# Decay products on four row groups, modulation sums in later blocks, and linear attention's first inputs loaded during neighbourhood attention

## The reference

```python
shift_x, scale_x, gate_x = jnp.split(silu_c @ w_ada[l] + b_ada[l], 3, axis=-1)   # modulation
...
def gla_log_decay(z, w_a, b_a):              # z: (B, L, 16), w_a: (16, 192)
    g = (z @ w_a + b_a).astype(jnp.float32)
    return split_heads(jax.nn.log_sigmoid(g) / GLA_TAU, GLA_HEADS)
...
def step(state, inp):                        # gated linear attention, chunks of 64 tokens
    qi, ki, vi, gi = inp
    b = jnp.cumsum(gi, axis=2)
    q_dec, k_dec = qi * jnp.exp(b), ki * jnp.exp(-b)
    a = jnp.where(tri, jnp.einsum('bhtk,bhsk->bhts', q_dec, k_dec), 0.0)
    o = jnp.einsum('bhts,bhsv->bhtv', a, vi) + jnp.einsum('bhtk,bhkv->bhtv', q_dec, state)
    ...
```

## Time and profile before

| | us |
|---|---|
| median of three executions | 4718.71 |
| the profiled execution | 4721.0 |
| its span | 4719.2 |
| TensorE busy | 4208.3 (89%) |
| VectorE busy | 2202.5 (47%) |
| ScalarE busy | 1482.8 (31%) |
| GpSimd busy | 465.4 (10%) |

### The profile page before, as it was taken

How to read it: one execution, slowest core, us unless ns; L and a number is a source line. 1 busy time by engine, 2 the same in 40 slices (tenths; PEclk the granted TensorE clock), 3 DMA queues, 4 the chain that set the end, 5 groups by cost and what they waited for, 6 DMA issues and landing times. The chain is left out here.

```text
span 4719.2 us, 67376 instructions
## 1 busy us (share of the span) xinstructions
PE 4208.3 (89%) x25867; PEld 3358.5 (71%) x25867; DVE 2202.5 (47%) x4748; ACT 1482.8 (31%) x3341; POOL 465.4 (10%) x497
## 2 busy tenths in 40 slices
PE   7999999799669899999979956959999989979799
PEld 4777789577457778778857745847777767758687
DVE  5553111266656553111126665853831256657554
ACT  4001333156412220144316631431111257641211
POOL 3111000200000030000020000031420000100100
PEclk9999999999759999999989976979999999989899
DMA  4343121710325442212180043532111123346321
GB/s 179 118 132 112 72 72 54 262 42 13 127 101 200 171 151 69 94 72 72 58 273 14 14 151 125 219 148 78 63 65 64 61 84 118 96 156 256 116 75 64
DMA packets 230291, 520.88 MB, mean 110 GB/s; under 512 B 46587, under 2 KB 100747, under 8 KB 220627
## 3 DMA queue, kind: packets, MB, share of 16 engines
q1 hardware_dynamic: 206068, 434.47, 25.9%
q0 software_dynamic: 23904, 82.11, 4.8%
HBM read 320.07 MB, written 196.43 MB: 109 GB/s over the span
## 5 line engine op out<-in xcount | busy, mean ns | idle before, releaser
L72 PE MATMUL tm_tacc<-tm_tw_hi,hT_hi 128*128 128x384 f32 (+1 forms) x1120 | 418.6, 374 | 1.6 <-POOL tm_tw_lo L916 1.6
L73 PE MATMUL tm_tacc<-tm_tw_lo,hT_hi 128*128 128x384 f32 (+1 forms) x1120 | 413.4, 369 | 0.0
L74 PE MATMUL tm_tacc<-tm_tw_hi,hT_lo 128*128 128x384 f32 (+1 forms) x1120 | 413.3, 369 | 0.0
L72 PE MATMUL tz_tacc<-tz_tw_hi,hT_hi 128*128 128x512 f32 x896 | 359.8, 402 | 24.4 <-DVE tz_tw_lo L892 12.8
L72 PE MATMUL cm_acc<-hT_hi,cm_wb_hi 128*128 128x512 f32 (+1 forms) x912 | 362.0, 397 | 0.0
L73 PE MATMUL tz_tacc<-tz_tw_lo,hT_hi 128*128 128x512 f32 x896 | 356.1, 397 | 0.0
L74 PE MATMUL tz_tacc<-tz_tw_hi,hT_lo 128*128 128x512 f32 x896 | 356.1, 397 | 0.0
L74 PE MATMUL cm_acc<-hT_hi,cm_wb_lo 128*128 128x512 f32 (+1 forms) x912 | 344.0, 377 | 0.0
L73 PE MATMUL cm_acc<-hT_lo,cm_wb_hi 128*128 128x512 f32 (+1 forms) x912 | 343.5, 377 | 0.0
L804 DVE SCALAR_TENSOR_TENSOR tm_ds<-tm_dg,tm_ds 128x512 f32<-128x512 f32 (+1 forms) x40 | 25.6, 639 | 531.8 <-ACT tm_ds L798 531.8
L72 PEld LDWEIGHTS tm_tacc<-tm_tw_hi,hT_hi 128*128 128x128 f32 x1120 | 213.6, 191 | 56.5 <-ACT tm_tz L940 23.2
(11 more groups left out here) (370 smaller groups left out, 8801.2 us busy)
## 6 DMA issues: line engine op xcount, KB each, us to landing
scr_z<-tz_tz SPq DMA_DIRECT2D x112, 256.0 KB, 2.0
scr_zcm<-cm_zo SPq DMA_DIRECT2D x96, 256.0 KB, 2.0
scr_ztm<-tm_tz SPq DMA_DIRECT2D x68, 256.0 KB, 2.0
out_mx<-scr_mix SPq DMA_DIRECT2D x34, 512.0 KB, 3.6
out_gt<-scr_ztm SPq DMA_DIRECT2D x34, 512.0 KB, 4.5
scr_xres<-out_x POOLq DMA_DIRECT2D x34, 512.0 KB, 4.1
scr_z<-out_xn POOLq DMA_DIRECT2D x34, 512.0 KB, 4.7
cm_area<-in_w_ada POOLq DMA_DIRECT2D x64, 256.0 KB, 3.1
```

The source lines that it names most:

```text
L72: nc.tensor.matmul(out, ah, bh, start=start, stop=False)
L73: nc.tensor.matmul(out, ah, bl, start=False, stop=False)
L74: return nc.tensor.matmul(out, al, bh, start=False, stop=stop)
```

## The change

There are three parts.

1. `DecaySums`: the four products of a segment (two directions, two groups of heads) are issued together, each on its own 16 rows starting at partitions 0, 32, 64 and 96, into four banks. `pe` does so only at the first unit of a segment. Rank rows and weights lie twice on the partitions for it. Units stand one tile later (`+ 1` in `at`). The rank rows of the next segment are loaded after the first store of a segment. `load` asks for the rank rows first.
2. `Modulation`: it starts at block 26 with a period of 4 blocks instead of block 9 with 6, so its steps come after the rotated chunks. Three blocks of a period have 3, 3 and 2 steps; before, four blocks had 2 each. The row is added in the same block as the first steps.
3. `LinearInputs`: decay sums and keys of group 0 and all values are loaded into memory set aside at the right end, by SP in `neighbourhood_phase`, between the stores of output tiles 1 and 2. `gla_phase` loads the rest: queries of group 0 first, then the mask, then group 1.

```diff
 class Modulation:
-        self.start, self.period = 9, 6
+        self.start, self.period = 26, 4
...
     def dve(self, dve, n):
         j, p = (n - self.start) // self.period, (n - self.start) % self.period
-        if p == 2 and 1 <= j <= self.NG:
+        if p == 1 and 1 <= j <= self.NG:
             self.row(dve, j - 1)
-        if 0 <= j < len(self.chunks) and p >= 2:
-            self.step(dve, j, 2 * p - 4)
-            self.step(dve, j, 2 * p - 3)
+        if 0 <= j < len(self.chunks) and p >= 1:
+            for k in range(3 * p - 3, min(3 * p, KC)):
+                self.step(dve, j, k)
...
 class DecaySums:
-        self.at = {sum(tiles[:c]) + 3 * j: 5 * c + j for c in range(4) for j in range(5)}
+        self.at = {sum(tiles[:c]) + 3 * j + 1: 5 * c + j for c in range(4) for j in range(5)}
...
     def ranks(self, sp, seg):
         a, w = 512 * seg, min(512, LT - 512 * seg)
         if seg:
-            sp.wait_ge(self.g_mm, 4 * seg)
-        for d in range(2):
-            sp.dma_start(self.z[32 * d:32 * d + RANK, 0:w], rank_rows(self.io)[d, :, a:a + w]).then_inc(self.z_in, 16)
+            sp.wait_ge(self.g_mm, seg)
+        for j in range(4):
+            sp.dma_start(self.z[32 * j:32 * j + RANK, 0:w], rank_rows(self.io)[j % 2, :, a:a + w]).then_inc(self.z_in, 16)
...
     def store(self, sp, u):
...
-        if u % 4 == 3 and u < 19:
+        if u % 4 == 0 and u < 16:
             self.ranks(sp, u // 4 + 1)
 
     def pe(self, pe, u):
-        hh, d, a, w = self.place(u)
+        if u % 4:
+            return
         if u == 0:
-            pe.wait_ge(self.c_in, 48)
+            pe.wait_ge(self.c_in, 64)
         else:
             pe.wait_ge(self.g_ev, u)
-        pe.wait_ge(self.z_in, 32 * (u // 4 + 1))
-        self.nc.tensor.matmul(self.bank[:, 0:w], self.wa[32 * d:32 * d + RANK, hh * 128:(hh + 1) * 128],
-                              self.z[32 * d:32 * d + RANK, 0:w], start=True, stop=True).then_inc(self.g_mm, 1)
+        pe.wait_ge(self.z_in, 64 * (u // 4 + 1))
+        w = self.place(u)[3]
+        for j in range(4):
+            last = self.nc.tensor.matmul(self.bank[j][:, 0:w], self.wa[32 * j:32 * j + RANK, :], self.z[32 * j:32 * j + RANK, 0:w], start=True, stop=True)
+        last.then_inc(self.g_mm, 1)
...
 def neighbourhood_phase(nc, l, io, keep, na, pre):
...
                 for i, t in enumerate(tiles):
+                    if i == 2:
+                        pre.load(sp, io)
                     sp.wait_ge(o_ev, i + 1)
...
 def gla_phase(nc, l, io, keep, wo, pre):
...
-                for hh in range(2):
-                    sp.dma_start(qd[hh][0][:, :], decay_sums(io, hh, 0)).then_inc(b_in[hh][0], 16)
...
+                sp.dma_start(q[0][:, 0:LQ], io["zcm"][8, :, 0:LQ]).then_inc(q_in[0], 16)
+                for cc in range(2):
+                    sp.dma_start(mask[64 * cc:64 * cc + 64, :, :],
+                                 io["gla_mask"][64 * cc:64 * cc + 64, :, 64 * cc:64 * cc + 64]).then_inc(m["cst_in"], 16)
+                sp.dma_start(qd[1][0][:, :], decay_sums(io, 1, 0)).then_inc(b_in[1][0], 16)
+                sp.dma_start(k[1][:, :], io["zcm"][11, :, :]).then_inc(k_in[1], 16)
+                sp.dma_start(qd[1][1][:, :], decay_sums(io, 1, 1)).then_inc(b_in[1][1], 16)
+                sp.dma_start(q[1][:, 0:LQ], io["zcm"][9, :, 0:LQ]).then_inc(q_in[1], 16)
...
+class LinearInputs:
...
+    def load(self, sp, io):
+        sp.dma_start(self.sums[0][:, :], decay_sums(io, 0, 0)).then_inc(self.sums_in[0], 16)
+        sp.dma_start(self.k[:, :], io["zcm"][10, :, :]).then_inc(self.keys_in, 16)
+        sp.dma_start(self.sums[1][:, :], decay_sums(io, 0, 1)).then_inc(self.sums_in[1], 16)
+        sp.dma_start(self.v[:, :, :], io["ztm"][:, 1024 + D_NA:TM].rearrange("(t p) c -> p t c", p=128)).then_inc(self.values_in, 16)
```

More of the change, by code:

```diff
@@ L743, in __init__ @@
         self.nc, self.l, self.io = nc, l, io
-        self.z, self.wa, self.ba = P.sb("dz", [64, 512]), P.sb("dwa", [64, 256]), P.sb("dba", [128, 4])
+        self.z, self.wa, self.ba = P.sb("dz", [128, 512]), P.sb("dwa", [128, 128]), P.sb("dba", [128, 4])
         self.start, self.g, self.s = P.sb("dstart", [128, 512]), P.sb("dg", [128, 512]), P.sb("ds", [128, 512])
-        self.bank = P.ps("dbank")
+        self.bank = [P.ps(f"dbank{j}") for j in range(4)]
         (self.c_in, self.z_in, self.g_mm, self.g_ev, self.ln_ok, self.b_ok, self.b_out) = [P.sem(n) for n in (
             "dc_in", "dz_in", "dg_mm", "dg_ev", "dln_ok", "db_ok", "db_out")]
-        self.at = {sum(tiles[:c]) + 3 * j: 5 * c + j for c in range(4) for j in range(5)}
+        self.at = {sum(tiles[:c]) + 3 * j + 1: 5 * c + j for c in range(4) for j in range(5)}
     def place(self, u):
@@ L757, in ranks @@
         if seg:
-            sp.wait_ge(self.g_mm, 4 * seg)
-        for d in range(2):
-            sp.dma_start(self.z[32 * d:32 * d + RANK, 0:w], rank_rows(self.io)[d, :, a:a + w]).then_inc(self.z_in, 16)
+            sp.wait_ge(self.g_mm, seg)
+        for j in range(4):
+            sp.dma_start(self.z[32 * j:32 * j + RANK, 0:w], rank_rows(self.io)[j % 2, :, a:a + w]).then_inc(self.z_in, 16)
     def load(self, sp):
         l, io = self.l, self.io
-        sp.dma_start(self.wa[:, :], io["w_alpha"][l:l + 1, :, :].rearrange("a p n -> p (a n)")).then_inc(self.c_in, 16)
+        self.ranks(sp, 0)
+        for hh in range(2):
+            sp.dma_start(self.wa[64 * hh:64 * hh + 64, :], io["w_alpha"][l:l + 1, :, hh * 128:(hh + 1) * 128].rearrange("a p n -> p (a n)")).then_inc(self.c_in, 16)
         sp.dma_start(self.ba[:, :], io["b_alpha"][l:l + 1, :, :].rearrange("a p n -> p (a n)")).then_inc(self.c_in, 16)
         sp.dma_start(self.start[:, :], io["chunk_start"][:, 0:512]).then_inc(self.c_in, 16)
-        self.ranks(sp, 0)
     def store(self, sp, u):
@@ L1376, in gla_phase @@
         q = [P.sb(f"q{j}", [128, LT]) for j in range(2)]
-        k = [P.sb(f"k{j}", [128, LT]) for j in range(2)]
-        v = P.sb("v", [128, NT, GH * GDV])
-        qd = [wo.buf[0:2], [P.sb(f"qd1{d}", [128, LT]) for d in range(2)]]
+        pre.beside(P)
+        k = [pre.k, P.sb("k1", [128, LT])]
+        v = pre.v
+        qd = [pre.sums, [P.sb(f"qd1{d}", [128, LT]) for d in range(2)]]
         kd = [wo.buf[2:4], [P.sb(f"kd1{d}", [128, LT]) for d in range(2)]]
@@ L1404, in steps_needed @@
             return max(order[0].index(2 * n + 1), order[1].index(2 * n))
-        names = ("cst_in", "v_in",
+        names = ("cst_in",
                  "ls_ok", "exp_q", "exp_k", "qd_ok", "kte_ok", "kt_mm", "kt_ev", "u_mm", "s_ok", "a_mm", "a_ok", "o_mm", "o_ok")
         m = {n: P.sem(n) for n in names}
-        b_in = [[P.sem(f"b{hh}{d}_in") for d in range(2)] for hh in range(2)]
-        q_in, k_in = [[P.sem(f"{n}{hh}_in") for hh in range(2)] for n in ("q", "k")]
+        b_in = [pre.sums_in, [P.sem(f"b1{d}_in") for d in range(2)]]
+        q_in, k_in = [P.sem(f"q{hh}_in") for hh in range(2)], [pre.keys_in, P.sem("k1_in")]
         o_out = [P.sem(f"o_out{j}") for j in range(2)]
@@ L1653, in _, with __init__, place, behind @@
                     values_out(NO + n)
+class LinearInputs:
+    def __init__(self, P, nc):
+        self.sums_in = [P.sem(f"sums{d}_in") for d in range(2)]
+        self.keys_in, self.values_in = P.sem("keys_in"), P.sem("values_in")
+        self.nc = nc
+    def place(self, P):
+        self.sums = self.behind(P, "sums")
+        self.k, self.v = self.beside(P)
+    def behind(self, P, name):
+        return [self.nc.alloc_sbuf_tensor(f"{P.name}_{name}{d}", [128, LT], F32, side="right") for d in range(2)]
+    def beside(self, P):
+        return (self.nc.alloc_sbuf_tensor(f"{P.name}_k0", [128, LT], F32, side="right"),
+                self.nc.alloc_sbuf_tensor(f"{P.name}_v", [128, NT, GH * GDV], F32, side="right"))
+    def load(self, sp, io):
[3 more added lines that the diff above has]
+        sp.dma_start(self.v[:, :, :], io["ztm"][:, 1024 + D_NA:TM].rearrange("(t p) c -> p t c", p=128)).then_inc(self.values_in, 16)
 class OutputWeights:
-    def __init__(self, P):
-        self.buf = [P.sb(f"buf{j}", [128, LT]) for j in range(4)]
+    def __init__(self, P, pre):
+        self.buf = pre.behind(P, "buf") + [P.sb(f"buf{j}", [128, LT]) for j in (2, 3)]
         self.raw = [self.buf[k // 2][:, (k % 2) * D:(k % 2 + 1) * D] for k in range(KC)]
@@ L2840, in first_layer @@
                            [512, 512, 384, 384], [ACT.Silu] * 2 + [ACT.Copy] * 2, tiles, decays=DecaySums(P, nc, l, io, tiles))
-    with phase(nc, f"nain{l}") as P:
-        na = Neighbourhood(P, last)
-        fourier_phase(nc, l, io, keep, na)
-        neighbourhood_phase(nc, l, io, keep, na)
-    with phase(nc, f"wo{l}") as P:
-        wo = OutputWeights(P)
-        gla_phase(nc, l, io, keep, wo)
-        out_phase(nc, l, io, keep, wo)
+    with phase(nc, f"pre{l}") as Q:
+        pre = LinearInputs(Q, nc)
+        with phase(nc, f"nain{l}") as P:
+            na = Neighbourhood(P, last)
```

(7 more changed lines are left out.)

19 lines of the change are left out of this document (5 added, 14 removed).

## The result

Four executions of the changed kernel took 4635.1 to 4649.8 us, median 4641.7. The kernel before, run beside it, took 4718.4 (median of four). The ratio is 0.9835 (95% interval 0.9804 to 0.9865): 76.6 us faster, where 72.0 were forecast. The profiled execution is the longest of the four, 4649.8 us with a span of 4647.9, so the two traces differ by only 71.3 us.

What follows compares the result with a forecast made beforehand. TensorE bounds projections and neighbourhood attention, a ScalarE-VectorE-TensorE chain linear attention. Terms 26.9 + 16.8 + 8 + 20.3 = 72.0 us off the median 4718.7 give 4646.7 us; range 4632 to 4668.

Steps and rivals of the forecast that it cites:

- Part 1, packs: Projection stages: a pack of four decay products costs 1.3 us, about one single unit; 26.9 us gained over both layers.
- The start: Start of each token projection: first tile goes ahead of the decay unit and ends 1.0 us earlier per layer.
- The boundaries of the chunks: Projections, three units per layer: TensorE still waits for the weight split, which doesn't move; 3.75 us counted as not gained.
- Part 1, rank rows: Projections: waits for late rank rows and the low clock behind them go; 16.8 us gained, at least 9.
- Part 2: Modulation in the first layer's channel projection: later steps remove waits and low clock; 8 us gained, bounds 0 and 12.
- The wait ahead of block 31: Modulation, first chunk: two rotations and a short block make TensorE wait about 3 us.
- The later waits: Modulation, reductions after the first: TensorE waits 0 to 0.3 us at each.
- The 15 us to be won: Channel projection, blocks 9 to 59: 15 us of waits and low clock, nearly all in blocks 15 to 33.
- Part 3: Linear attention's inputs: chain of states starts 10.7 and 9.6 us earlier in the two layers; 20.3 us gained, at least 12.
- Cover: Early loads under neighbourhood attention, DMA engines used for 9%: they cost nothing; bounds 0 and 8 us per layer.
- Rivals 1 to 5: 1 packs paired/in-turn 0.12; 2 modulation gains nothing 0.09; 3 loads delay attention 0.08; 4 start given back 0.07; 5 slower 0.02.
- The fifth: Modulation: weights land one at a time, a step takes some 5 us, kernel slower at 4813 us; chance 0.02.

## Why the prediction was right, point by point

- **Part 1, packs: 26.9 forecast, 30.8 measured** (the changed kernel against single products with early rows, one trace each). The core was right: a unit gives back 1.25 us and a pack costs 1.26 or 1.27. The start was mis-sized. The first tile ends 2.5 and 2.6 us earlier behind the stage's start (against the kernel before 1.8 and 2.2), where 1.0 was forecast: 3.1 us more in the two layers. The boundaries of the chunks, forecast as unchanged, held in the first layer but for 0.4 us (tiles 17 and 18 take 13.28 us after and 13.25 before, tiles 53 and 54 10.75 and 10.73). In the second layer they cost 2.3 us more at two of three and 0.3 less at the third, as VectorE's scan delays the split; the forecast took it for granted that the split doesn't move. The last part, 2.6 us, isn't the change's: plain tiles of 384 columns take 4.16 or 4.24 us, in either kernel, and the trace with single products has more of the latter. Errors of both signs cancel here in part.
- **Part 1, rank rows: 16.8 forecast, 15.5 measured** by the kernel that has this edit alone; its two starts are 1.1 us longer, without which it would be 16.6. That the loss hangs on the wait and not on the unit held: with the waits gone, no half clock stands behind a single unit. But how much clock a wait costs differs between executions. In the second execution of the kernel before the same four places lose 13.9 us, as the two waits of 2.3 us in its second layer have no half clock behind them at all:

```profile
2200.91 1.09 PE L783 MATMUL tm_dbank<-tm_dz,tm_dwa 16*128 16x512 f32 x2 [2.35 <-DMA tm_dz<-scr_branch]
...
2200.90:2208.70 7.80, 7.79 (x41) 7.04 (x42) 0.00 (x0) 2.16 (x4) 0.00 (x0) 1.00 0.07 25
```

- **Part 2: 8 forecast, 5.9 between the two traces.** The wait ahead of block 31 is 2.8 us by the weight loads, 3 was forecast. The later waits were laid out as 0 to 0.3 us each and came out at 0.6, 1.3 and 1.3, and the low clock as one or two stretches of 1.7, where there are three of 1.4. The second of these sizes is not a property of the order: in the second execution two such stretches are left, one behind the wait ahead of block 31 and one at block 51, and the stage takes 373.2 us. Old orders took 380.2 to 383.5 us in six traces (mean 382.3), the new one 373.0 to 375.4 in six (mean 374.2): 8.1 us. The 15 us to be won were not nearly all in blocks 15 to 33, as the forecast had it: block 40, which takes 7.36 us without wait and low clock, took 10.24.
- **Part 3: 20.3 forecast, 10.9 + 8.6 = 19.5 measured** in the start of the chain, and 26.9 in the stages. It goes through to the stage's end. The surplus of 7.4 us lies behind the start of the chain, where two executions of one kernel differ by up to 9.4 us with the clock of the output products; the forecast held that stretch to be unchanged.
- **Cover.** That the early loads cost nothing in neighbourhood attention held, with four times as many too.
- **The untouched branch** of the second block took 5.4 us more in this trace; over all traces here it has 351.3 to 364.2 us. With the surplus of linear attention it is of the size of what two executions of one kernel differ by, which is why the sum of terms (about 72 to 74 us) is a better account of the change than the 71.3 us between two spans. That the whole time came out within 5 us of the forecast is in part luck: the terms are off by up to 4 us each, and the surplus of linear attention and the losses of the untouched stages, which no term has, nearly cancel. Rivals 1 to 5 did not happen. The fifth, weights one at a time, is excluded by the waits in the trace: first steps wait 4.9 to 5.8 us three times, and the other 112 instructions of the steps 12.6 us in all.

## What to carry to other kernels

Products on few rows are worth gathering on four row groups, as a pack cost here what one of them costs; but have its inputs there early, since a pack asks for all of them at once. When units move by a tile, look at what every engine that serves them has next in its list: here VectorE was late with the next weights. Loads moved under a stage that used the DMA engines for 9% were free, also when they raised this to 36%, and what such a load is worth is read from the first instruction that waits for it to the head of the next chain. Judge an edit of a few microseconds by its stage over several traces, not by the whole time.

## What was not expected of the hardware

- Sixteen one-column products in a row (1.95 us) can be followed by 3.4 us at half clock (0.50) though TensorE never idles: in the seven traces with reductions ahead of their blocks in the new order, ahead of block 47 it happened in one and ahead of block 55 in three. Ahead of block 51, where a wait of 1.3 to 1.5 us stands in front of them, it happened in all seven (once it began during them). Between main products it was not seen. The Trainium skill ("TensorE: Matmul & The Clock Gate", Part 1) says of the ramp at a kernel's start that it varies between runs of one kernel. The traces here show the same of places in the middle of a kernel.
- The clock of a stretch with short products differs that way too: 0.53 and 0.83 for the same 508 products, 8.6 us apart.
- How much half clock follows a wait of TensorE differs too. In two executions of the kernel before, a wait of 2.3 to 2.4 us for rank rows was followed by 6.8 and 3.4 us of it at one place, and by 3.4 us and none at another. Packs in turn on the same 16 rows lowered the clock in seven of eight wide packs without any idle time ahead of them.
